# Recurrence of a hybrid trunk: inverse products on the quadrants beside the diagonal, between the squares

## What is computed

```python
def _rwkv_step(S, xs):
    r, w, k, v, kk, a = xs
    sa = jnp.einsum('bhij,bhj->bhi', S, -kk)
    S = S * w[:, :, None, :] + sa[..., None] * (kk * a)[:, :, None, :] + v[..., None] * k[:, :, None, :]
    return S, jnp.einsum('bhij,bhj->bhi', S, r)
```

## Time and profile before

| | us |
|---|---|
| median of 3 runs (2724.72 to 2727.78) | 2727.39 |
| profiled execution, its own time | 2721.46 |
| its span in the profile | 2719.4 |
| recurrence, from the first squares of the first step (384.85) to the end of the last | about 320 |
| a step in the first 15 | 15.2 to 17.0 |
| a step in the last five | 13.9 to 14.8 |

### The profile page before, as it was taken

One profiled execution on the slowest core, in us unless ns is written; L12 is line 12 of the kernel. 1 busy time (PEld: TensorE's weight loads), 2 busy tenths in 40 slices (PEclk: granted clock), 3 DMA queues, 4 the chain that ended last, 5 costly groups with the idle time before them and its releaser, 6 DMA issues. The chain is left out here.

```text
span 2719.4 us, 52138 instructions
## 1 busy us (share of the span) xinstructions
PE 2486.5 (91%) x19059; PEld 2166.9 (80%) x19059; DVE 1607.8 (59%) x2330; ACT 1391.2 (51%) x2117; POOL 395.6 (15%) x571
## 2 busy tenths in 40 slices
PE   6998969999889999899799788888999999999993
PEld 4887958778578888788677788777999999999992
DVE  3255566665752232223311688547888888888885
ACT  4225655554323333212222566417888788787873
POOL 1133122221141000011200343042000000000002
PEclk8998989999999999999899899888999999999996
DMA  7530000000541222223254000319999999999994
GB/s 271 203 127 3 18 5 3 3 3 3 197 157 47 77 73 74 77 78 124 79 214 147 31 16 13 120 50 342 381 388 380 387 380 382 383 377 385 376 383 190
DMA packets 262845, 472.23 MB, mean 174 GB/s; under 512 B 29436, under 2 KB 202108, under 8 KB 256548
## 3 DMA queue, kind: packets, MB, share of 16 engines
q1 hardware_dynamic: 255200, 445.69, 46.5%
q0 software_dynamic: 4416, 14.70, 1.4%
q10 hardware_dynamic: 3076, 9.71, 0.9%
HBM read 453.54 MB, written 16.48 MB: 173 GB/s over the span
## 5 line engine op out<-in xcount | busy, mean ns | idle before, releaser
L3379 DVE TENSOR_TENSOR m_lo<-m_raw,m_hi 128x1408 fp32r<-128x1408 f32 (+1 forms) x459 | 648.4, 1457 | 64.8 <-ACT m_hi L3238 62.5
L3238 ACT ACTIVATE m_hi<-m_raw 128x1408 fp32r<-128x1408 f32 (+1 forms) x459 | 548.6, 1246 | 41.8 <-DMA m_raw<-moe_w_gu 27.3
L195 DVE TENSOR_TENSOR w_lo<-w_raw,w_hi 128x1024 fp32r<-128x1024 f32 (+1 forms) x132 | 162.1, 1231 | 485.3 <-ACT w_hi L190 484.7
L213 PE MATMUL acc<-w_hi,h_hi 128*128 128x512 f32 (+1 forms) x1120 | 431.9, 386 | 18.0 <-PEq L2798 9.4
L215 PE MATMUL acc<-w_hi,h_lo 128*128 128x512 f32 (+1 forms) x1120 | 424.9, 379 | 0.0
L214 PE MATMUL acc<-w_lo,h_hi 128*128 128x512 f32 (+1 forms) x1120 | 424.7, 379 | 0.0
L190 ACT ACTIVATE w_hi<-w_raw 128x1024 fp32r<-128x1024 f32 (+1 forms) x134 | 135.0, 1014 | 457.2 <-PE acc L215 401.9
L213 PEld LDWEIGHTS acc<-w_hi,h_hi 128*128 128x128 f32 x1120 | 213.1, 190 | 79.1 <-issue 33.8
L215 PEld LDWEIGHTS acc<-w_hi,h_lo 128*128 128x128 f32 x1120 | 212.9, 190 | 34.5
L214 PEld LDWEIGHTS acc<-w_lo,h_hi 128*128 128x128 f32 x1120 | 213.3, 190 | 32.6
L3156 PE MATMUL p_gates<-m_hi,x_hi 128*128 128x352 f32 x544 | 181.7, 334 | 5.0 <-issue 5.0
(11 more groups left out here) (407 smaller groups left out, 4959.8 us busy)
## 6 DMA issues: line engine op xcount, KB each, us to landing
m_raw<-moe_w_gu SPq DMA_DIRECT2D x544, 352.0 KB
m_raw<-moe_w_dn SPq DMA_DIRECT2D x187, 512.0 KB
ada_w<-ada_w SPq DMA_DIRECT2D x40, 1024.0 KB, 4.9
w_raw<-ffn_w_gu SPq DMA_DIRECT2D x88, 256.0 KB, 2.9
w_raw<-w_in_o SPq DMA_DIRECT2D x24, 512.0 KB, 5.7
w_raw<-ffn_w_dn SPq DMA_DIRECT2D x22, 512.0 KB, 3.6
w_raw<-w_in_e SPq DMA_DIRECT2D x28, 384.0 KB, 5.0
scratch_y_slots<-y_slot ACTq DMA_DIRECT2D x18, 512.0 KB, 6.3
```

Of the source, the lines that this page charges most:

```text
L195: eng.tensor_tensor(lo, self.raw_of(c, k), hi, ALU.subtract).then_inc(self.lo.sem, 1)
L213: eng.matmul(out, hi, whi[:, b, :], start=first, stop=False)
L3238: a.activation(whi[:, u % MSPLIT, 0:size(u)], raw[:, s, 0:size(u)], ACT.Copy).then_inc(s_hi.sem, 1)
L3379: dve.tensor_tensor(wlo[:, u % MSPLIT, 0:n], raw[:, u % MRAW, 0:n], whi[:, u % MSPLIT, 0:n], ALU.subtract).then_inc(s_lo.sem, 1)
```

## The change

`level_pe` is rearranged by direction. For each direction it first takes both waits (copy and add), then issues for each head the squares and, behind them, the inverse products. The inverse product of operand half b now writes the other half of PSUM, `HALVES[1 - n]`, so it uses the quadrants (0,1) and (1,0). Since the sum then has its operands in different halves, the add is split into two instructions of 64 partitions each.

```diff
-            def square_pe(pe, ct, i, d, l):
+            def squares_ready(pe, ct, i, d, l):
                 q, s, c, par = unit(ct, i, d)
-                pA = pU[d][:, 0, :]
...
-                for hh in range(2):
-                    for form in ((0, 1) if l < LEVELS - 1 else (1,)):
-                        for b in HALVES:
-                            xt, x = (AM[b, par, d, hh, b] if l == 0 else X[b, l % 2, d, hh, 0, :]), X[b, l % 2, d, hh, 1, :]
-                            at = (2 * hh + form) * HD
-                            mm = pe.matmul(pA[b, at:at + HD], *((xt, x) if form else (x, xt)), start=True, stop=True)
-                mm.then_inc(u_sq[d].sem, 1)
-
-            def inverse_pe(pe, ct, i, d, l):
+
+            def square_pe(pe, ct, i, d, l, hh, form):
                 q, s, c, par = unit(ct, i, d)
-                pI = pU[d][:, 1, :]
+                at = (2 * hh + form) * HD
+                for b in HALVES:
+                    xt, x = (AM[b, par, d, hh, b] if l == 0 else X[b, l % 2, d, hh, 0, :]), X[b, l % 2, d, hh, 1, :]
+                    mm = pe.matmul(pU[d][b, 0, at:at + HD], *((xt, x) if form else (x, xt)), start=True, stop=True)
+                return mm
+
+            def inverse_ready(pe, ct, i, d, l):
...
-                for hh in range(2):
-                    for b in HALVES:
-                        mm = pe.matmul(pI[b, hh * HD:(hh + 1) * HD], X[b, l % 2, d, hh, 1, :], TF[b, par, d, hh, :], start=True, stop=True)
-                mm.then_inc(u_iv[d].sem, 1)
+
+            def inverse_pe(pe, ct, i, d, l, hh):
+                q, s, c, par = unit(ct, i, d)
+                for n, b in enumerate(HALVES):
+                    o = HALVES[1 - n]
+                    mm = pe.matmul(pU[d][o, 1, hh * HD:(hh + 1) * HD], X[b, l % 2, d, hh, 1, :], TF[b, par, d, hh, :], start=True, stop=True)
+                return mm

             def level_pe(pe, ct, i, l):
-                if l < LEVELS:
-                    for d in range(2):
-                        square_pe(pe, ct, i, d, l)
+                forms = (0, 1) if l < LEVELS - 1 else (1,)
                 for d in range(2):
+                    if l < LEVELS:
+                        squares_ready(pe, ct, i, d, l)
                     if l:
-                        inverse_pe(pe, ct, i, d, l)
+                        inverse_ready(pe, ct, i, d, l)
+                    for hh in range(2):
+                        if l < LEVELS:
+                            for form in forms:
+                                sq = square_pe(pe, ct, i, d, l, hh, form)
+                        if l:
+                            iv = inverse_pe(pe, ct, i, d, l, hh)
+                    if l < LEVELS:
+                        sq.then_inc(u_sq[d].sem, 1)
+                    if l:
+                        iv.then_inc(u_iv[d].sem, 1)
...
-                out = TF[:, par, d]
-                dve.tensor_tensor(out, out, pU[d][:, 1, 0:P].rearrange("p (h n) -> p h n", h=2), ALU.add).then_inc(u_tt[d].sem, 1)
+                out, times = TF[:, par, d], pU[d][:, 1, 0:P].rearrange("p (h n) -> p h n", h=2)
+                for b, o in zip(HALVES, HALVES[::-1]):
+                    mm = dve.tensor_tensor(out[b], out[b], times[o], ALU.add)
+                mm.then_inc(u_tt[d].sem, 1)
```

## The result

The changed kernel takes 2740.26 us (median of 5 runs, 2737.35 to 2744.44) against 2727.35 for the kernel before beside it: 1.0047 times as long, 95% interval 1.0036 to 1.0059. That is slower by 0.5%, 12.9 us at the medians. The profiled execution took 2743.56 us, its span is 2741.7.

What follows compares the result with a forecast made beforehand. VectorE's chain from first mask to turn was taken as the bound in 15 of 20 steps. Terms 6.1 + 6.15 + 6.1 - 4.0 = +14.4 us gave 2735.9 profiled, plus 5.9 to the median: 2741.8; range 2730 to 2750.

Steps and rivals of the forecast that it cites:

- Products hidden: TensorE, levels 1 to 4: moved inverse products run under the squares, 0.46 us less per level, 37 us of issue time.
- Halves at 0.32: VectorE's adds: split halves start 0.32 us apart, so four take 1.27 us a level.
- (a): Last five steps, without preparation of a next tile: gain 0.8 us a step, 4.0 in all.
- (b): Six steps with a scan: first mask unmoved, 0.98 us lost between the masks; loss 1.0 each, 6.1 in all.
- (c): Six steps with products of the next tile: loss 1.17 us in one kind, 0.88 in the other, 6.15 together.
- (d): Three steps with reciprocals: 0.98 us counts twice, loss 1.87 each, a further 0.5 in the first; 6.1 together.
- The rival that products aren't hidden: TensorE in the recurrence: last five steps gain nothing, VectorE's costs stay; about 19 us more, 2746.5; chance 0.15.
- the one that TensorE is the bound everywhere: Recurrence: adds hide in VectorE's 124 us of idle time; up to 28 us less, 2699; chance 0.03.
- The overlap of halves: VectorE's adds: halves start 0.20 us apart, extra 0.39 a level; 6.4 us less, 2721.0; chance 0.08.

Runs made afterwards that it cites:

- experiment 2: Kernel before with each add split into two of 64 partitions, products unmoved: 2742.22 us against 2726.44 for the kernel before, ratio 1.0058.
- experiment 1: Changed kernel with whole 128-partition adds, so its output is not the reference's: 2714.56 us against 2726.44 for the kernel before, ratio 0.9959.
- experiment 3: Changed kernel's order of waits and instructions, but products on the old quadrants and whole adds: 2724.58 us against 2726.44 for the kernel before, ratio 0.9994.
- experiment 4: Changed kernel with the backward direction's two half adds in opposite order: 2739.64 us against 2726.44 for the kernel before, ratio 1.0050.
- experiment 5: Changed kernel with 32 superfluous square instructions ahead of a wait in the three steps with reciprocals: 2736.08 us against 2726.08 for the kernel before.
- experiment 6: Changed kernel, backward half adds reversed, 32 superfluous squares in reciprocal steps, 16 before the turn in the first 15 steps: 2727.29 us against 2726.08 before.
- 7: Changed kernel with whole adds (output not the reference's) and all squares of a level before its products: 2714.56 us against 2726.08 for the kernel before.
- experiment 9: Moved products and reversed half adds only at some levels of last-tile and scan steps, GpSimd's product later: 2714.74 us against 2726.08 for the kernel before.

## Why the prediction was right, and where its steps were off

It was right in sign and size, 2741.8 forecast and 2740.26 measured, and its mechanism is shown: experiment 2 puts the cost on the halves, experiment 1 the gain on TensorE, experiment 3 excludes the order. But terms of the sum were off and partly offset one another, so how close it came is luck in part. The forecast was +14.4 us for the recurrence; the trace has +16.7.

**Products hidden.** Right: the link behind a level's 48 instructions begins 0.98 us after the first of them.

**Halves at 0.32.** Nearly: 0.307 between starts, so four span 1.20 where 1.27 was taken. The spacing goes with the partitions where a half starts, not with its width (experiment 4).

**(a) Last five, -4.0.** Measured -2.7. From mask to mask 2.54 us against 2.55 forecast. The first mask comes 0.32 earlier in its step (657.92 in a step from 652.07) where 0.46 was taken, which makes -0.67 in such a step. The last of the five has no turn behind it and gains 0.1: it was counted like the others, wrongly.

**(b) Scan, +6.1.** Measured +4.5, of which 1.55 is extra in the first of them, whose first 4.0 us lie in the first fall of the clock. The other five have +0.5 instead of +1.0, made of two changes that were not foreseen. The halves moved the centring to 505.25, where GpSimd's product (503.87, 1.55 us long) is nearly over, and it takes 0.85 instead of 1.68 us, so the masks are 3.25 apart (before 3.15) and not 4.1. Against that, `half_end` now lies beside another GpSimd instruction and takes 0.71 instead of 0.17, and the first mask is late by 0.37. `half_end` and GpSimd's product before, then GpSimd after:

```profile
489.42 0.17 DVE L2155 TENSOR_SCALAR half_end<-L 128x5 f32<-128x5 f32 x1
492.33 1.54 POOL L2166 TENSOR_TENSOR iclr<-iclr,kk 128x640 f32<-128x640 f32 x1
...
501.42 0.87 POOL L2162 TENSOR_SCALAR kd<-iclr,channel_vectors 128x640 f32<-128x640 f32 x1 [12.70 <-ACT iclr L2144]
...
503.87 1.55 POOL L2166 TENSOR_TENSOR iclr<-iclr,kk 128x640 f32<-128x640 f32 x1
```

The centring ends 2.23 us after the start of that product in both kernels (494.56 and 506.10), though it starts 0.55 behind it before and 1.38 after. In experiment 1 it starts 0.22 behind and takes 2.00, which gives 2.22:

```profile
490.87 1.54 POOL L2166 TENSOR_TENSOR iclr<-iclr,kk 128x640 f32<-128x640 f32 x1
491.09 2.00 DVE L2174 TENSOR_TENSOR L_centred<-L,half_end 128x640 f32<-128x640 f32 x1
```

GpSimd set the end of the centring, so the later start that the halves gave it cost nothing.

`half_end` started at 501.62 and ended at 502.33, just after this one's end at 502.29. The Trainium skill (SBUF — State Buffer, who interferes with whom) says that VectorE and GpSimd share a pair of ports, that whichever issues first holds it for its whole instruction while the other waits, and that a VectorE instruction takes part if both its inputs lie in SBUF or if it runs in a two-port mode. The centring, with two inputs in SBUF, agrees. The time of `half_end`, with one, agrees too, but no row shows in which mode it ran. The prediction did not ask what the moved VectorE instructions would meet on GpSimd.

**(c) Products of the next tile, +6.15.** Measured +4.3: +0.86 and +0.56 for 1.17 and 0.88. In the third step (from 512.68) the masks are 3.21 apart against 3.25 forecast, but the first comes only 0.55 later in its step where 0.80 was taken; the halves' spacing makes up 0.14 of that. The two masks, after:

```profile
520.41 1.21 DVE L2485 TENSOR_TENSOR a_masked<-p_build,masks 128x1024 f32<-128x1024 f32 x1
...
523.62 1.23 DVE L2485 TENSOR_TENSOR a_masked<-p_build,masks 128x1024 f32<-128x1024 f32 x1
```

**(d) Reciprocals, +6.1.** This term failed most: +10.6. VectorE's part was right where it can be seen alone (1.75 in experiment 5, 1.87 forecast). What was missing is TensorE's clock, a term that the sum put at nothing without a reason: it took 1.00 for granted while it forecast more idle time for TensorE. The clock accounts for 2.05 us in each of two steps by experiment 5. In the first two steps of the first tile, experiment 6 without a fall has 17.39 and 17.21, against 18.94 and 18.89 here; only a part of this difference is the turned halves, and no run splits it exactly.

So about 7 us of clock, which no term held, stand for about 6 that VectorE's terms in (b) to (d) had too much (3.1, 1.9 and an estimated 0.9), and (a) gave 1.3 less. Of the 7, 4.1 is shown by experiment 5, 1.55 is the first scan step's excess over the other five, and the rest, in the first step, is an estimate from experiment 6. The rest of the closeness is the base, and it is luck: the forecast added 5.9 us between the profiled time and the median of before, while the profiled execution after lies 3.3 above its median. For that execution the forecast was 2735.9, and it took 2743.56: 2.3 us of the miss lie in the recurrence, the rest outside it. The trace has +16.7 in the recurrence and the medians +12.9. In every experiment but the first, too, the recurrence comes out worse against before than the median does, by 1.0 to 3.8 us (2.8, 2.4 and 2.4 in experiments 2, 4 and 5, 3.1 in 6 and 7, 3.8 in 9); why stays open. Runs of one kernel differ along with their mean granted clock: of the 17 of the kernel before beside experiments 1 to 4, the fastest has 2720.54 us at 0.963 and the slowest 2731.70 at 0.957.

The rival that products aren't hidden and the one that TensorE is the bound everywhere are excluded by the timelines and by experiments 1 and 2. The overlap of halves holds only for the pair on equal partitions, which this change doesn't issue.

## What to carry to other kernels

Where two engines alternate as the bound, cost a trade between them stage by stage: what the faster one saves is worth nothing in a stage that ends on the other. Here the same edit, with GpSimd's move, is worth -11.3 us (-7.6 in the recurrence) where it is confined to such places (experiment 9), and +12.9 everywhere.

When a change leaves TensorE waiting longer, look at its granted clock and price a fall, and when it shifts VectorE, look at what GpSimd does beside it. An edit that needs instructions on half the partitions costs VectorE a whole instruction for each half: 286 ns for a 64x128 add, 281 for a 128x128 one.

## What the runs showed of the hardware

- TensorE's granted clock fell to 1.2 GHz for 6.8 us after idle times of 1.14 and 0.70 us close together in a step that was otherwise busy, and 32 instructions put into the first of them kept it at 2.4 GHz: 20.79 us became 18.74. In the first tile the same 32 did not prevent a fall.
- A VectorE instruction whose neighbour starts on the same partitions starts 0.205 us after it, on other partitions 0.29 to 0.32, at equal size (64x128, 0.28 us each).
- 128x640 with two inputs in SBUF takes VectorE 0.82 us. Beside a GpSimd product of 1.54 us that is under way as it starts it ends 2.22 to 2.23 us after the start of that product: it takes 0.85, 1.68 or 2.00, by when it starts.
- TensorE starts an instruction for free quadrants ahead of some six that were issued before it (26 of 32 squares had begun).
